# Low parts of three layer norms moved from VectorE to GpSimd, with ScalarE's two writes interleaved

## The reference

```python
def layer_norm(x, g, b):
    mu = jnp.mean(xf, axis=-1, keepdims=True)
    var = jnp.mean(jnp.square(xf - mu), axis=-1, keepdims=True)
    y = (xf - mu) * lax.rsqrt(var + LN_EPS) * g + b

for i in range(DEPTH):
    mix = gated_deltanet(h, ...) if i % N_MIXERS == 0 else short_conv_mixer(h, ...)
    h = layer_norm(ALPHA * h + mix, ln_mix_g[i], ln_mix_b[i])
    h = layer_norm(ALPHA * h + conv_ffn(h, ...), ln_ffn_g[i], ln_ffn_b[i])
```

## Time and profile before

| what | value |
|---|---|
| median of 3 runs | 1270.98 us (1270.62 to 1271.13) |
| profiled execution, its own time | 1270.44 us |
| its span, first to last instruction | 1268.8 us |
| TensorE busy | 1243.1 us, 98% of the span |
| VectorE busy | 987.6 us, 78% |
| ScalarE busy | 693.2 us, 55% |
| GpSimd busy | 53.8 us, 4% |
| mean granted TensorE clock | 0.997 of full |

### The profile page before, as it was taken

The page is one execution under the profiler, slowest core; times in us unless marked ns, Lnnn a source line. Parts: engine busy times, 40 slices in busy tenths (PEclk is TensorE's granted clock), DMA queues, the critical chain, the costliest instruction groups (busy, mean ns, idle before and its releaser), DMA issues.

```text
span 1268.8 us, 28526 instructions
## 1 busy us (share of the span) xinstructions
PE 1243.1 (98%) x10313; PEld 1201.5 (95%) x10313; DVE 987.6 (78%) x1801; ACT 693.2 (55%) x1134; POOL 53.8 (4%) x93
## 2 busy tenths in 40 slices
PE   8999999999999999999999999999999999999997
PEld 8998898999999999999998999998999999999986
DVE  6898469988978998998876887765677668877653
ACT  6876546655633544655544655554465566555542
POOL 0002000000001000000000000000000000000000
PEclk9999999999999999999999999999999999999999
DMA  7541225788888587588865366665455336656650
GB/s 274 154 130 35 85 68 167 263 270 275 304 274 283 203 297 236 178 299 270 290 223 163 101 208 184 185 211 172 139 172 193 117 117 183 192 185 185 216 182 34
DMA packets 64201, 244.71 MB, mean 193 GB/s; under 512 B 7136, under 2 KB 7424, under 8 KB 64128
## 3 DMA queue, kind: packets, MB, share of 16 engines
q1 hardware_dynamic: 53472, 204.77, 49.0%
q0 software_dynamic: 10656, 38.93, 10.1%
HBM read 242.63 MB, written 1.05 MB: 192 GB/s over the span
## 4 chain that ended last, share of the span: by engine, by line
PE 87%; DVE 8%; ACT 3%; issue 1%; DMA 1%; DVEq 0%; ACTq 0%; SPq 0%
PE ps L1841 20%; PE ps L1840 20%; PE ps L1842 19%; PE ps L2201 8%; PE ps L2202 4%; DVE wlo L417 2%; DVE tb L1090 2%; PE ps L1855 2%; PE ps L1856 2%; PE ps L1861 1%; DMA raw<-in_w_a_in 1%; PE ps L2347 1%; PE ps L2349 1%; PE ps L2348 1%; PE ps L2046 1%
## 5 line engine op out<-in xcount | busy, mean ns | idle before, releaser
L410 ACT ACTIVATE whi<-raw 128x1024 fp32r<-128x1024 f32 (+1 forms) x360 | 400.3, 1113 | 295.4 <-PE ps L1842 173.1
L1840 PE MATMUL ps<-hhi,whi 128*128 128x258 f32 (+4 forms) x1952 | 557.4, 286 | 3.1 <-DVE hlo L1068 2.0
L1841 PE MATMUL ps<-hlo,whi 128*128 128x258 f32 (+4 forms) x1952 | 555.7, 285 | 0.0
L1842 PE MATMUL ps<-hhi,wlo 128*128 128x258 f32 (+4 forms) x1952 | 550.2, 282 | 0.0
L417 DVE TENSOR_TENSOR wlo<-raw,whi 128x1024 fp32r<-128x1024 f32 (+1 forms) x360 | 463.5, 1293 | 79.1 <-ACT whi L410 74.4
L1840 PEld LDWEIGHTS ps<-hhi,whi 128*128 128x128 f32 x1952 | 370.0, 190 | 5.3 <-DVE wlo L417 3.9
L1842 PEld LDWEIGHTS ps<-hhi,wlo 128*128 128x128 f32 x1952 | 371.5, 190 | 0.0
L1841 PEld LDWEIGHTS ps<-hlo,whi 128*128 128x128 f32 x1952 | 370.0, 190 | 0.3
L2201 PE MATMUL ps<-aboth,whi 128*128 128x512 f32 x462 | 161.8, 395 | 0.0
L2202 PE MATMUL ps<-aboth,wlo 128*128 128x256 f32 x462 | 129.4, 280 | 0.0
L2201 PEld LDWEIGHTS ps<-aboth,whi 128*128 128x128 f32 x462 | 86.7, 188 | 20.1
(11 more groups left out here) (425 smaller groups left out, 1527.0 us busy)
## 6 DMA issues: line engine op xcount, KB each, us to landing
raw<-in_w_up SPq DMA_DIRECT2D x176, 512.0 KB, 4.1
raw<-in_w_down SPq DMA_DIRECT2D x64, 704.0 KB, 4.3
ring<-in_ada_w POOLq DMA_DIRECT2D x72, 512.0 KB, 5.5
raw<-in_w_mix SPq DMA_DIRECT2D x48, 512.0 KB, 3.5
raw<-in_w_a_in SPq DMA_DIRECT2D x32, 512.0 KB, 3.7
raw<-in_w_b_cx SPq DMA_DIRECT2D x16, 512.0 KB, 4.9
raw<-in_w_a_out SPq DMA_DIRECT2D x8, 512.0 KB, 3.6
raw<-in_w_b_gate SPq DMA_DIRECT2D x8, 512.0 KB, 4.5
```

What stands on the lines that cost most here:

```text
L410: nc.scalar.activation(whi[:, s, 0:blocks * P], raw[:, s, 0:blocks * P], ACT.Copy).then_inc(hi_split, 1)
L1840: nc.tensor.matmul(out, whi[:, s, w], rhi(k0 + k), start=first and k == 0, stop=False)
L1841: nc.tensor.matmul(out, whi[:, s, w], rlo(k0 + k), start=False, stop=False)
L1842: ins = nc.tensor.matmul(out, wlo[:, s, w], rhi(k0 + k), start=False, stop=last and k == blocks - 1)
```

## The change

The low parts of norms 0, 1 and 2 leave VectorE. GpSimd writes them as `hf - hhi`, so each waits for the residual tile. For this ScalarE no longer writes the eight rounded tiles and then the eight residual tiles, but each residual tile right behind its rounded tile. GpSimd's program has the three groups of eight subtractions among its DMA issues: the first ahead of the two first ring loads, the second after ada load 37, the third after ada load 51; the loop of ada loads is cut in three for that. Norm 5 (`rms1`) keeps its low parts on VectorE.

```diff
@@ gpsimd
+            def norm_lows(i, version, n):
+                for m in range(KT):
+                    pool.wait_ge(hf_ready, i * KT + m + 1)
+                    nc.gpsimd.tensor_tensor(hlo[:, m, 0:n], hf[:, m, 0:n], hhi[:, m, 0:n], ALU.subtract).then_inc(rhs_ready, 1)
+
+            norm_lows(0, "ln0", N_A)
             pool.wait_ge(tiles_read, SLOTS + PH["up0"].first)
             for o in range(2):
                 pool.dma_start(ring[:, o, :], io["ada_w"][o]).then_inc(ld_ada[o], 16)
-            with pool.Fori(1, ADA_OPS // 2) as i:
...
+            ada_loads(1, ADA_AT["b_cx"] // 2)
+            norm_lows(1, "ln1", N_F0)
+            ada_loads(ADA_AT["b_cx"] // 2, ADA_AT["up1"] // 2 + 1)
+            norm_lows(2, "ln2", N_B)
+            ada_loads(ADA_AT["up1"] // 2 + 1, ADA_OPS // 2)
@@ scalar, act_norm
                         nc.scalar.activation(hhi[:, m, 0:n], xb[:, m, 0:n], ACT.Identity, bias=shift(m)).then_inc(rhs_hi, 1)
+                        if i < 3:
+                            nc.scalar.activation(hf[:, m, 0:n], xb[:, m, 0:n], ACT.Identity, bias=shift(m)).then_inc(hf_ready, 1)
...
-                if i < 4:
+                if i == 3:
@@ vector, dve_norm
-                if version:
+                if i == 5:
                     for m in range(KT):
                         dve.wait_ge(rhs_hi, RHS_AT[version] + m + 1)
```

More of the change, by code:

```diff
@@ L510, in _, with ada_loads @@
                 pool.dma_start(ring[:, o, :], io["ada_w"][o]).then_inc(ld_ada[o], 16)
-            with pool.Fori(1, ADA_OPS // 2) as i:
-                for o in range(2):
-                    pool.wait_ge(ada_done, i * 2 + (o - 1))
-                    pool.dma_start(ring[:, o, :], io["ada_w"][i * 2 + o]).then_inc(ld_ada[o], 16)
+            def ada_loads(i0, i1):
+                with pool.Fori(i0, i1) as i:
+                    for o in range(2):
+                        pool.wait_ge(ada_done, i * 2 + (o - 1))
+                        pool.dma_start(ring[:, o, :], io["ada_w"][i * 2 + o]).then_inc(ld_ada[o], 16)
+            ada_loads(1, ADA_AT["b_cx"] // 2)
[3 more added lines that the diff above has]
+            ada_loads(ADA_AT["up1"] // 2 + 1, ADA_OPS // 2)
             pool.wait_ge(tiles_read, SLOTS + PH["mix"].first)
@@ L820, in act_norm @@
                         nc.scalar.activation(hhi[:, m, 0:n], xb[:, m, 0:n], ACT.Identity, bias=shift(m)).then_inc(rhs_hi, 1)
+                        if i < 3:
+                            nc.scalar.activation(hf[:, m, 0:n], xb[:, m, 0:n], ACT.Identity, bias=shift(m)).then_inc(hf_ready, 1)
                 if i == 3:
                     nc.scalar.activation(hhi[:, :, SEQ:N_SH], shifts(0), ACT.Copy)
-                if i < 4:
+                if i == 3:
                     for m in range(KT):
                         act.wait_ge(y_ready, Y_AT[i] + m + 1)
-                        if i == 3:
-                            nc.scalar.activation(hhi[:, m, 0:n], xb[:, m, 0:n], ACT.Identity, bias=small[:, SHIFT_A + m:SHIFT_A + m + 1],
-                                                 scale=a_of(0)(m)).then_inc(rhs_hi, 1)
+                        nc.scalar.activation(hhi[:, m, 0:n], xb[:, m, 0:n], ACT.Identity, bias=small[:, SHIFT_A + m:SHIFT_A + m + 1],
+                                             scale=a_of(0)(m)).then_inc(rhs_hi, 1)
                         nc.scalar.activation(hf[:, m, 0:n], xb[:, m, 0:n], ACT.Identity, bias=shift(m)).then_inc(hf_ready, 1)
```

## The result

| what | before | changed |
|---|---|---|
| median | 1270.98 us (1270.56 to 1271.54, 7 runs) | 1275.41 us (1273.51 to 1276.64, 7 runs) |
| ratio | | 1.0034, interval 1.0025 to 1.0044 |
| profiled execution, its span | 1268.8 us | 1273.7 us, its time 1275.41 |
| TensorE busy | 98% of the span | 98% |

The change makes the kernel slower by 4.4 us, 0.34%; the interval of the ratio stands for 3.2 to 5.6 us. The prediction was 1274.5, that is 3.5 slower. The direction and the place are right, and 0.9 us of the size is missing, which the medians alone could not tell from noise. The profile can: it has a term that the prediction had not, a fall of TensorE's granted clock behind norm 1.

The account below looks back on a forecast made before the run. TensorE, 98% busy, was taken to wait at norms 0 to 2 for the last low part. 0.47 + 0.25 + 2.36 + 0.47 = 3.55 us on 1270.44 gave 1273.99, with 0.54 for the median 1274.5; range 1271.3 to 1276.4.

Parts of the forecast that it names:

- What bounds it: Norms 0 to 2: TensorE's eighth low load follows the last low part by about 0.06 us, so that end sets the price.
- The relief is worth nothing: Norms 0 to 2: VectorE loses 3.3 us in each, but TensorE waits for none of the work behind, so no gain.
- The rival in which the relief pays: Stand before the eighth low load: 0.38 us a norm, at best 1.1 us gained, time 1269.9; chance 0.04.
- The pairs: ScalarE's rounded and residual tiles interleaved, 0.81 us a pair; the interleaving alone costs 0.1 us in a norm.
- GpSimd's speed: GpSimd's subtractions of 262 columns take 0.74 us each, less than a pair of 0.81, so GpSimd would follow ScalarE.
- Turns, one instruction each: GpSimd and VectorE alternate when both read two SBUF tensors: last low part 0.47 us later in norms 0 and 2, 2.36 in norm 1.
- The rival in which only the split blocks: Norm 1: ada products do not block GpSimd, 1.89 us less, sum 1.66, time 1272.6; chance 0.14.
- The ring loads: After norm 0: first ring load issues at 223.2, lands 5.5 us later, VectorE waits 1.9 us, costing TensorE 0.25 us more.
- The bound of the range: First ring load after norm 0: a landing of 4.7 us costs TensorE nothing, one of 6.4 some 1.2 us.
- The sum of 3.55: Whole kernel: 0.47 for norm 0, 0.25 for ring loads, 2.36 for norm 1, 0.47 for norm 2, in us.
- The step "norm 1 is 2.36 later": End of norm 1: split and two ada products alternate with GpSimd's tiles; last low part at 424.73 against 422.37.

Follow-up runs that it names:

- the shared version: Changed kernel, but GpSimd makes low parts of tiles 0 and 1, VectorE waits, then makes six; ring loads precede low parts: 0.63 and 1.88 us below the kernel before.
- the kernel in which the ada products wait: Changed kernel, but in norm 1 VectorE's two ada products wait for GpSimd's eight low parts, its split does not: 0.88 us over the kernel before.
- the ring loads first: Changed kernel with GpSimd's two first ring loads moved ahead of its low parts of norm 0: 4.85 us over the kernel before, ratio 1.0035.
- norm 1 only: GpSimd's low parts and ScalarE's pairs in norm 1 alone, norms 0 and 2 as before: 2.72 us over the kernel before, ratio 1.0023.

## Why the prediction was right, and where it fell short

- **What bounds it.** Right. TensorE's eighth low load follows the last low part of the norm by 0.05 to 0.06 in every norm of the changed kernel, and TensorE waits for GpSimd (2.2 us in norm 1) and not for ScalarE's tiles.
- **The relief is worth nothing.** Right: VectorE's time went into waits, 3.28 us for ScalarE's copy of the tap after norm 0. The rival in which the relief pays allowed 1.1 us at best, near the 0.9 that the shared version gains.
- **The pairs.** Predicted pitch 0.81 and 0.1 a norm; measured 0.81, and 0.12 to 0.15. The low loads were to begin at 222.06 and did at 222.16, in a norm that began 0.10 later.
- **GpSimd's speed.** Predicted 0.74, under the pair of 0.81. Right in effect: undisturbed, its eight take 6.41, which is seven pairs of 0.81 and one subtraction of 0.74, and the disturbed ones 1.64 to 1.72, where 1.5 to 1.9 was forecast.
- **Turns, one instruction each.** Right. Norm 0: predicted 0.47, measured 0.44, with a split of 1.71 where the working had 1.70. Norm 2: 0.47 against 0.44 to 0.46. Norm 1: 2.36 against 2.40; tile 7 was to end at 424.73 and ended at 425.35 - 0.58 = 424.77. The rival in which only the split blocks (sum 1.66) was the costliest doubt, and the kernel in which the ada products wait shows what it would have been.
- **The ring loads.** Wrong, 0.25 for nothing (the step's own figures give 231.42 - 231.21 = 0.21). The 5.5 us of the earlier trace rows is the median of two loads, 4.7 and 6.4, and the first, the only one that mattered, had taken 4.7 already in the trace of before. In the changed kernel it landed 4.4 us after its issue at 223.24, and the ada product was due at 227.15, not 226.8: VectorE waited 0.60 instead of 1.9. The bound of the range, "with a landing of 4.7 nothing", was the case.
- **The missing term.** The sum of 3.55 should have been 3.3 for the waits (0.44 + 2.40 + 0.46), and then something that no step held: after the stands of norm 1 the granted clock falls to half in some executions, 1.5 us each time. 3.3 without it and 4.8 with it frame both medians, 4.43 and 3.93. So the forecast lies somewhat nearer than its steps deserve: it holds 0.25 that did not come and lacks the clock. The trace of before had it to be seen, though not in a norm. Its windows near the start:

```profile
6.00:7.00 1.00, 0.00 (x0) 0.00 (x0) 1.00 (x2) 1.00 (x5) 0.00 (x0) 1.00 1.11 406
7.00:8.00 1.00, 0.56 (x4) 0.59 (x5) 1.00 (x4) 1.00 (x4) 0.00 (x0) 1.00 0.98 404
8.00:9.00 1.00, 1.00 (x7) 1.00 (x6) 1.00 (x5) 0.44 (x2) 0.00 (x0) 0.58 1.05 387
9.00:10.00 1.00, 1.00 (x6) 1.00 (x6) 0.80 (x4) 0.93 (x1) 0.00 (x0) 0.50 1.03 419
```

TensorE does nothing from 6 to 7 us, is busy for 0.56 of the next microsecond, and then goes at half the clock. The step "norm 1 is 2.36 later" put a stand of that size into TensorE's work and gave it no other price than its length.

## What to carry to other kernels

Moving work to an idle engine is not free when that engine and the one relieved both read SBUF twice: the two take turns, and where the result is on the path, each instruction that the relieved engine brings forward holds the other up by most of its length (0.97 of 1.22 us for each ada product here, and 0.66 to 0.68 for the split). Ask what the relieved engine will do in the time that it gains, and if nobody wants that work, make it wait: that left 0.6 to 0.8 us of the 4.4 by the medians, 0.35 by the stretches. The little that was to be had came from splitting the job by time, GpSimd taking the tiles that were ready while VectorE worked out of PSUM.

Where a change puts waits like these (0.7 and 1.5 us) into TensorE's work, count their length and, with a chance, the slower products behind them.

## What the runs showed of the hardware that was not expected

- **The clock after a stand is not settled by the kernel.** With stands of 0.67 to 0.69 and 1.48 to 1.49 us in norm 1, the granted clock fell to 0.50 (1.2 GHz) behind them in three of five profiled executions (two of three of the changed kernel, the one with the ring loads first; not in the one with norm 1 only). It cost 1.5 us wherever it came there. In none of the nine without these stands did it fall there. After the stands of 0.3 us in norms 0 and 2 it fell in none. Near the start of the program, at 8 to 11 us, the same fall stands in seven of the fourteen profiled executions, that of the kernel before among them and the first of the changed kernel not, so there too it comes and goes; the one with the ring loads first also has one at 113 to 116 us.
- **A blocked instruction looks long, not late.** The turn shows as 1.71 to 1.77 for a VectorE instruction of 1.22 and as no idle time at all on either engine; the page's busy time counts it as work. GpSimd's eight subtractions read as 6.4, 7.1 or 9.0 us of busy time, with none, one or three of VectorE's two-input instructions beside them; single ones as 0.75 or 1.64 to 1.72.
